# First layer: two more parts of the modulation are multiplied on VectorE instead of TensorE

## What is computed

```python
c_act = jax.nn.silu(c)
for l in range(DEPTH):                      # 2 layers
    mod = c_act @ w_mod[l] + b_mod[l]       # (1024,) @ (1024, 6144)
    sh_m, sc_m, g_m, sh_f, sc_f, g_f = split(mod, 6)
    h = rms_norm(x, norm_mix_g[l]) * (1.0 + sc_m) + sh_m
    x = x + g_m * mixer(h, ...)             # three branches, gates, merge, w_out
    h = rms_norm(x, norm_ffn_g[l]) * (1.0 + sc_f) + sh_f
    x = x + g_f * moe_ffn(h, ...)           # 64 experts, top 8, and a shared one
```

## Time and profile before

| what | value |
|---|---|
| median of 3 runs | 2428.65 us |
| the profiled execution, its own time | 2426.65 us |
| its span in the profile | 2425.3 us |
| TensorE (PE) busy | 2311.0 us, 95% |
| VectorE (DVE) busy | 814.7 us, 34% |
| ScalarE (ACT) busy | 569.8 us, 23% |
| GpSimd (POOL) busy | 135.9 us, 6% |
| DMA mean | 278 GB/s |
| chain that ended last | PE 83%, DMA 11% |

### The profile page before, as it was taken

One profiled execution on the slowest core, in us unless ns is written; L12 is line 12 of the kernel. 1 busy time (PEld: TensorE's weight loads), 2 busy tenths in 40 slices (PEclk: granted clock), 3 DMA queues, 4 the chain that ended last, 5 costly groups with the idle time before them and its releaser, 6 DMA issues.

```text
span 2425.3 us, 34598 instructions
## 1 busy us (share of the span) xinstructions
PE 2311.0 (95%) x14027; PEld 1656.5 (68%) x14027; DVE 814.7 (34%) x2133; ACT 569.8 (23%) x1231; POOL 135.9 (6%) x179
## 2 busy tenths in 40 slices
PE   7999999999998988999999999998979999999998
PEld 4868896666666655768887676666647777754764
DVE  0476623222121211485524122211213543421264
ACT  2234302111110102134211111111113333321254
POOL 4040000000000000100000000000000000000110
PEclk9999999999999998999999999999989999999999
DMA  9785676999999996855776999999993454141300
GB/s 338 287 295 177 246 296 235 384 414 413 414 415 416 415 412 217 301 191 193 278 299 252 384 414 417 414 414 418 412 374 98 146 168 129 70 147 52 139 1 18
DMA packets 206908, 673.23 MB, mean 278 GB/s; under 512 B 14000, under 2 KB 74648, under 8 KB 156816
## 3 DMA queue, kind: packets, MB, share of 16 engines
q1 hardware_dynamic: 200064, 656.87, 70.1%
q0 software_dynamic: 6240, 13.99, 1.7%
q10 hardware_dynamic: 432, 0.01, 0.0%
HBM read 661.38 MB, written 9.45 MB: 277 GB/s over the span
## 4 chain that ended last, share of the span: by engine, by line
PE 83%; DMA 11%; ACT 2%; SPq 2%; DVE 1%; issue 1%; ACTq 0%; DVEq 0%
PE ps L278 47%; PE ps L2166 11%; PE ps L2201 6%; DMA ring<-in_w 6%; DMA ar<-in_w 5%; PE ps L2217 3%; PE ps L1748 3%; PE ps L1198 1%; SPq L570 1%; PE ps L686 1%; PE ps L2849 1%; PE ps L3462 1%; DMA ring<-in_w_in 1%; PE ps L3627 1%; PE ps L3610 1%
## 5 line engine op out<-in xcount | busy, mean ns | idle before, releaser
L278 PE MATMUL ps<-hT,ring 128*128 128x256 f32 (+2 forms) x2352 | 543.4, 387 | 3.2 <-ACT ar L1568 1.9
L278 PEld LDWEIGHTS ps<-hT,ring 128*128 128x128 f32 (+1 forms) x2352 | 440.1, 190 | 101.2 <-issue 38.0
L2166 PE MATMUL ps<-ring,ar 128*32 128x256 f32 (+2 forms) x2752 | 312.1, 386 | 38.1 <-DMA ring<-in_w 27.1
L2166 PEld LDWEIGHTS ps<-ring,ar 128*32 128x32 f32 (+2 forms) x2752 | 190.0, 124 | 145.6 <-issue 57.9
L2166 PE MATMUL ps<-ar 128*64 128x256 f32 (+2 forms) x1104 | 202.8, 394 | 13.6 <-DMA ar<-in_w 12.0
L2484 DVE SCALAR_TENSOR_TENSOR exact_parts<-ps,ar,exact_parts 128x512 fp32r<-128x512 f32 x100 | 75.1, 751 | 250.3 <-ACT exact_parts L2329 244.7
L2201 PE MATMUL ps<-ring,ar 128*32 128x512 f32 (+2 forms) x680 | 148.9, 617 | 5.4 <-DMA ring<-in_w 5.2
L2166 PEld LDWEIGHTS ps<-ar 128*64 128x64 f32 (+2 forms) x1104 | 118.8, 134 | 38.5 <-issue 19.9
L2460 DVE TENSOR_TENSOR ar<-ar,ps 128x256 f32<-128x256 f32 x50 | 21.1, 421 | 358.7 <-PE ps L2166 358.7
L278 PE MATMUL ps<-ring,ar 128*128 128x512 f32 x320 | 140.4, 596 | 0.0
L2329 ACT ACTIVATE exact_parts<-ps,ar 128x512 fp32r<-128x512 f32 x100 | 68.8, 688 | 240.2 <-PE ps L2201 222.1
(11 more groups left out here) (463 smaller groups left out, 2857.4 us busy)
## 6 DMA issues: line engine op xcount, KB each, us to landing
ring<-in_w SPq DMA_DIRECT2D x257, 1024.0 KB, 17.8
ar<-in_w SPq DMA_DIRECT2D x104, 1024.0 KB, 19.8
ring<-in_w_mod SPq DMA_DIRECT2D x36, 2048.0 KB, 12.0
ring<-in_w_in SPq DMA_DIRECT2D x28, 2048.0 KB, 11.8
ring<-in_ab_w_in SPq DMA_DIRECT2D x47, 1024.0 KB, 10.8
cst<-in_w SPq DMA_DIRECT2D x23, 1024.0 KB, 16.9
ring<-in_w_out SPq DMA_DIRECT2D x4, 2048.0 KB, 10.4
ring<-in_ab_w_out SPq DMA_DIRECT2D x2, 4096.0 KB, 13.4
```

The lines of the kernel that those rows point to most:

```text
L278: ins = te.matmul(o, l, r, start=(first and i == 0), stop=(last and i == len(pairs) - 1), skip_group_check=lax)
L2166: ins = te.matmul(b[cols, 0:256], K.x_b[:, kk, in_pair(p, cols)], w[r][:, kk, :], start=(kk == 0), stop=(kk == 7))
```

## The change

In layer 0 parts 2 and 3 are no longer early parts on TensorE; they become direct parts on VectorE, in the first place of the list. So layer 0 has twelve direct half parts instead of eight. They are called H0 to H11 here: H0, H1 are part 2; H2, H3 part 3; H4, H5 part 4; H6, H7 part 5 of layer 0; H8, H9 part 0 and H10, H11 part 1 of layer 1. The eight half parts of before are H4 to H11 in this count. Layer 1 keeps its lists.

- TensorE: the two `pe_mod` behind "qc" and "qk" become the two mod2 parts; the second one behind "qk" and the one behind "vc" are gone. `pe_direct` runs for H0, H1, H2 beside the branches (the places of before), H3 and H4 behind projection 0, H5 and H6 behind projection 1, and H7 to H11 behind gate tiles 0, 2, 4, 6 and 7.
- VectorE: H0 to H3 beside the branches; in the merge two pieces per tile instead of one in branches 0 and 1 (H4 to H7), and H8 to H11 ahead of branch 2.
- ScalarE copies H3 to H6 ahead of the context's activations, the rest behind the gates.
- Ring: the four half parts of parts 2 and 3 move from the projections to the gates. From the third gate half on the order is: gate half, H2; gate half, H3; w_proj_a, H4, H5; w_proj_b, H6, H7; gate half, H8, H9; gate half, H10, H11; w_proj_c. Before it was: w_proj_a, one; w_proj_b, one; gate half, one; gate half, one; w_proj_c.

```diff
-    K.direct_kept = nc.dram_tensor("direct_kept", (8, D), F32).ap()
+    K.direct_kept = nc.dram_tensor("direct_kept", (10, D), F32).ap()
...
             if b > 1:
-                gate(l, b, ((6,), (7,)))
+                gate(l, b, ((8, 9), (10, 11)) if l == 0 else ((6,), (7,)))
             rows(("proj", l, b), I[n][l], 4, 2)
             if b < 2:
-                direct(l, (4 + b,))
+                direct(l, ((4, 5), (6, 7))[b] if l == 0 else (4 + b,))
...
 def early_parts(l):
     if l == 0:
-        return [("mod", 0, 2), ("mod2", 0, 0), ("mod2", 0, 1), ("mod", 0, 3)]
+        return [("mod2", 0, 0), ("mod2", 0, 1)]
...
 def direct_parts(l):
-    return [("mod", 0, 4), ("mod", 0, 5), ("mod", 1, 0), ("mod", 1, 1)] if l == 0 else [("mod", 1, j) for j in range(2, 6)]
+    return [("mod", 0, j) for j in range(2, 6)] + [("mod", 1, 0), ("mod", 1, 1)] if l == 0 else [("mod", 1, j) for j in range(2, 6)]
...
-EARLY_AT = ("qc", "qk", "qk", "vc"), ("ua", "ug", "qc", "qk")
+EARLY_AT = ("qc", "qk"), ("ua", "ug", "qc", "qk")
...
-DIRECT_MERGE = {1: (5,), 4: (6,), 7: (7,)}
+DIRECT_PROJ = ((3, 4), (5, 6)), ((3,), (4,))
+DIRECT_MERGE = {0: (7,), 2: (8,), 4: (9,), 6: (10,), 7: (11,)}, {1: (5,), 4: (6,), 7: (7,)}
+DIRECT_PIECES = 2, 1
...
         if br < 2:
-            yield from pe_direct(K, l, (3 + br,))
+            yield from pe_direct(K, l, DIRECT_PROJ[l][br])
...
-    pieces = dve_direct(K, l, range(4, 8))
+    pieces = dve_direct(K, l, range(4, 12))
...
         for k in range(8):
-            if br < 2:
+            for _ in range(DIRECT_PIECES[l] if br < 2 else 0):
                 yield from step(pieces)
```

More of the change, by code:

```diff
@@ L713, in early_parts, with direct_items @@
     if l == 0:
-        return [("mod", 0, 2), ("mod2", 0, 0), ("mod2", 0, 1), ("mod", 0, 3)]
+        return [("mod2", 0, 0), ("mod2", 0, 1)]
     return [("mod2", 0, 2), ("mod2", 1, 0), ("mod2", 1, 1), ("mod2", 1, 2)]
 def direct_parts(l):
-    return [("mod", 0, 4), ("mod", 0, 5), ("mod", 1, 0), ("mod", 1, 1)] if l == 0 else [("mod", 1, j) for j in range(2, 6)]
-def direct_items(l, ns=range(8)):
+    return [("mod", 0, j) for j in range(2, 6)] + [("mod", 1, 0), ("mod", 1, 1)] if l == 0 else [("mod", 1, j) for j in range(2, 6)]
+def direct_items(l, ns=range(12)):
     items = [(*key, q) for key in direct_parts(l) for q in range(2)]
     return [items[n] for n in ns if n < len(items)]
-EARLY_AT = ("qc", "qk", "qk", "vc"), ("ua", "ug", "qc", "qk")
+EARLY_AT = ("qc", "qk"), ("ua", "ug", "qc", "qk")
 def early_at(l, place):
@@ L841, in pe_direct, with direct_at @@
         K.pe.also("used", *item)
+def direct_at(l, item):
+    return len(direct_items(0)) * l + direct_items(l).index(item)
 def direct_place(l, item):
-    return (8 * l + direct_items(l).index(item)) % 3
+    return direct_at(l, item) % 3
 def act_direct(K, l, ns):
     for item in direct_items(l, ns):
-        n = 8 * l + direct_items(l).index(item)
+        n = direct_at(l, item)
         K.ac.wait_ge(*(yield ("direct_ps", *item)))
@@ L1725, in pe_merge @@
                     K.pe.also("used", "in", l, 4 + br, k // 4)
-                yield from pe_direct(K, l, DIRECT_MERGE.get(k, ()))
+                yield from pe_direct(K, l, DIRECT_MERGE[l].get(k, ()))
         w = k_major(K.flat["proj", l, br], D, 4)
@@ L1765, in act_merge @@
     ac.wait_ge(*K.act.all())
-    yield from act_direct(K, l, (3, 4))
+    yield from act_direct(K, l, DIRECT_PROJ[l][0] + DIRECT_PROJ[l][1])
     if l == 0:
@@ L1772, in act_merge @@
         ac.activation(K.sg[:, k, :], K.ps["gate_ps", l, 2, k][:, 0:256], ACT.Sigmoid).then_inc(*K.act("gate", l, 2, k))
-        yield from act_direct(K, l, DIRECT_MERGE.get(k, ()))
+        yield from act_direct(K, l, DIRECT_MERGE[l].get(k, ()))
 def dve_merge(K, l):
@@ L1829, in pool_merge @@
     K.ev["end", ("branches", l), "pool"] = K.pool.all()
-    yield from pool_direct(K, l, range(3, 8))
+    yield from pool_direct(K, l, range(3, 12))
 def moe_memory(K):
```

## The result

The kernel after took 2432.51 us, the median of 10 runs (2429.00 to 2435.78), against 2427.39 us of the kernel before on the same chip (2423.19 to 2431.71). The ratio is 1.0021 [1.0012, 1.003], so the change costs 5.1 us. The forecast was +4.4 us and "within 0.3%". Measured a second time, with new runs of both kernels, the ratio was 1.003 [1.0017, 1.0043]. The profiled execution of after took 2432.66 us, with a span of 2431.3.

A forecast was written before the change was run, and what follows sets the result against it. Through layer 0's projections, branches and merge, TensorE alone was taken as the bound. The terms -7.1 + 1.4 + 7.7 + 1.7 + 0.7 = +4.4 us on 2428.65 gave 2433.1 us, range 2422.5 to 2439.

The forecast's parts named there:

- Steps 1 and 3: Layer 0: two of four `pe_mod` leave TensorE, -7.1 us; VectorE's taps end in time for the earlier branches, cost 0.
- Step 2: TensorE in layer 0: four more short sums (`pe_direct`) at 0.36 us each, +1.4 us.
- Steps 5 and 6: Merge: VectorE ends branch 0 at 274.4, then waits for H6, landing at 282.4, 9.3 us after issue.
- the sum by the fit: Third rival: H6 lands in 6.8 us, stall 5.2, H11 not late; +1.2 us, 2429.9 us, chance 0.08.
- Step 7: Merge, projection 1 to gates: TensorE stalls for H6's eighth piece and banks VectorE has yet to read, +7.7 us.
- Step 8: TensorE's clock around the stall: a stretch at half clock, bounds 0 and 3.4 us, middle taken, +1.7 us.
- Step 9: End of the gates: H11 is done at 329.3, TensorE wants it at 328.6, +0.7 us.
- The second rival: End of the gates: H11 lands after 14.2 us and costs 4.9 us more; +9.3, 2438.0 us, chance 0.18.
- My first rival: Merge: VectorE's wait for H6 is hidden, so no stall comes; -5.7 us, 2423.0 us, chance 0.12.

The follow-up runs named there:

- e1: After, with H3's short sum (and ScalarE's copy) ahead of projection 0 instead of behind it; ratio to before 1.0016 [1.0005, 1.0026].
- e9: e8 with H0's and H1's sums behind the second q tile, H5's ahead of projection 0, H6's behind tile 1 of projection 1; ratio 0.998 [0.9971, 0.999].
- e2: After, with only an eighth of H6 loaded, so half of part 5 is not computed from its weights; one run, 2429.98 us (before 2424.03).
- e11: After, with twelve filler matmuls of 256 columns in TensorE's wait ahead of H6's sum; one run, 2433.48 us (before 2424.73).
- e3: After, with no VectorE pieces in branch 1, H6 to H11 done behind its tiles, H6's sum behind gate tile 1; one run, 2429.80 us (before 2424.03).
- e5: e1 with H5's sum also moved, to behind tile 2 of projection 1; ratio to before 1.0001 [0.999, 1.0011].
- e12: e9 with H0's sum behind the first q tile, H1's still behind the second; ratio to before 0.9982 [0.9972, 0.9993].
- e6: Before, with part 2 multiplied by VectorE in its gap in the projections, ring order kept, part 3 on TensorE; ratio 1.0015 [1.0006, 1.0024].
- e8: Before, with part 2 on VectorE in its projection gap and part 3 on VectorE beside branches and merge; ratio 1.0007 [0.9998, 1.0016].

## Why the prediction was right

| step | forecast | measured |
|---|---|---|
| 1. two `pe_mod` less, up to projection 0 | -7.1 | -7.5 |
| 2. four short sums | +1.4 | +1.6 |
| 7. stall | +7.7 | +7.8 |
| 8. clock | +1.7 | +1.5 |
| 9. H11 | +0.7 | +1.2 |
| sum | +4.4 | +4.6; A itself +4.7; runs +5.1 |

The mechanism is the one forecast. That the sum fits so well owes something to misses of 0.1 to 0.5 us that go both ways.

- **Steps 1 and 3.** Projection 0 began (251.36 - 36.42) - (258.66 - 36.27) = -7.45 us against before. Of this 7.0 us were there at the first scores; where the branches gained the rest was not looked into. The scores came at 163.44, where 163.6 was forecast. VectorE's taps ended in time; its wait for the scores was 0.39 us, the forecast room 0.3.
- **Step 2.** Two of the sums stand right behind another one and cost 0.22 us each (279.46 and 280.04 in e1 are 0.58 apart, one sum alone takes 0.36). The other two stand between gate tiles and cost 0.56 each: from the first gate tile to projection 2 it is 29.74 us in e9 with four sums, 29.18 in before with three.
- **Steps 5 and 6.** Branch 0 ended at 267.3, which is 274.4 on the clock of before. H6 landed 9.1 us after its issue (9.3 forecast), the load behind it after 15.1 (14.2 for the one in that place before). VectorE waited 7.53 us. By the fit of the Trainium skill's page "DMA: Bandwidth & Descriptors", section "Anatomy of one DMA", which is for GpSimd's path, the estimate for this load of SyncE's was 6.8 us; the trace does not agree (9.1), and the sum by the fit, +1.2 us, is below the interval of the measured ratio.
- **Step 7.** 24.28 - 16.48 (the same stretch with the same sums in e1, without a wait) = 7.8 us. TensorE waited 2.89 us at H6, 2.9 forecast. Not all of the stall is idle time, as the prediction has it: TensorE idled 5.75 us in three pieces instead of 7.7 in four, and the other 2 us are what the sum and the transposes took longer, at half clock. This changes nothing, since the end of the stall hangs on VectorE's reading of tile 6. e1 and e2 show that it was H6's load: with it early, the stall is gone.
- **Step 8.** 5.20 us instead of 3.72 for the gate tile: 1.5. That it is so near the middle is luck: in the repeat that tile lost 2.8. The forecast bounds 0 and 3.4 held both. Steps 8 and 9 are also not independent: with the tile at full clock, in e11, TensorE waited 2.03 us for H11 instead of 1.12.
- **Step 9.** H11 landed 9.8 us after its issue. TensorE idled 1.12 us; from the tile's start to the sum it was 4.84 us, where it is 3.65 without a wait (295.55 to 299.20 in e3), so 1.2. The term was too small: the landing took 0.5 us more than the 9.3 assumed. The second rival's landing of 14.2 did not come: H11 was the first of its pair.

**What the prediction did not see** changes nothing in the number but all in the remedy. My first rival ("the stall does not come") gave -5.7 us. With the stall taken away (e1, e2, e5) A was -0.5, +0.4 and -0.4. Behind H6 lay the gate half of 267.05, third in the queue, landed 19.8 us after its issue, at 286.9, and then the DMA queue as a whole. I had priced each load by its own slot and landing, and asked only who waits for H6 and H11. The sum of loads per stretch was in reach: the share of 258 to 368 us rose from 0.74 to 0.86, while that of 94 to 258 fell from 0.71 to 0.60.

Windows of after over these two stretches:

```profile
94.00:258.00 164.00, 163.01 (x851) 126.09 (x844) 107.31 (x250) 63.64 (x155) 29.30 (x15) 1.00 0.60 213
258.00:368.00 110.00, 103.12 (x508) 90.63 (x508) 60.12 (x112) 17.67 (x41) 8.37 (x15) 0.97 0.86 330
```

The change takes bytes from a stretch with room and gives them to one with little. The bound shows best from projection 1 to `w_out` alone: the share is 0.89 before, 0.98 in after, and 0.89 again in e9 and e12, which undo the shift for part 2, and gain.

**Open.** The times of e1 and e6 lie 3.9 and 3.6 us over before (intervals from 1.2 and 1.5), while their A is -0.5 and +0.4. Their traces do not show it: e1's is of the fastest of its ten runs (2424.18 us, the median is 2428.08), and behind the start of `w_out` it is 2.8 us shorter than that of before, e6's 1.3 us. What the rest is was not settled. Why e12's 2.3 us of A over e9 do not show in the runs is open too; the interval of either is some 5 us wide.

## What to carry to other kernels

Where weights come through a ring in strict order, a step that changes its engine changes when its slot is released: price the load that takes that slot, and then add up the loads of the whole stretch against its DMA share, since behind the first late load the next stands a few us away. Taking work into an idle gap without touching the order of loads, and releasing its slot as soon as its last reader can, gave here what the moved loads gave away. A wait's named releaser is worth a second look against what the code waits for: in e3 it was an instruction that only happened to end at the same moment as the load landed.

## What the runs showed of the hardware

- Three loads of 2 MB issued within 1.3 us of each other landed 9.1, 15.1 and 19.8 us after their own issues. In the full queue of e5 H10 took 18.5 us.
- What a pause costs in clock is not a constant. The granted clock fell to 0.50 behind pauses of TensorE of 2.03 us (e11), 2.89 (after), 3.17 (e8), 3.78 and 4.36 (e3), and the group at that clock took 1.5 to 1.8 us more. It stayed at 1.00 behind 2.81 us in e1, and in e6 behind the same 3.17 us as in e8. In the repeat of after it was still 1.00 behind 2.58 us, fell just behind the 0.83 us that followed, and cost the gate tile 2.8 us. The 2.24 us ahead of the router cost 1.7 us in the executions of before, e1 and e11 and nothing in the other eleven (3.64 us for the same 16 matmuls).
- Filler of 12 fp32 matmuls of 256 columns shows as 24 records and took 5.45 us.
